# Moving the e operand and the SwiGLU hidden layer by 64 bytes in on-chip memory

## The reference, cut to what matters

```
h = rmsnorm(x, g_ffn1);  x = x + 0.5 * ((silu(h @ w1_a) * (h @ w3_a)) @ w2_a)
h = rmsnorm(x, g_mix);   p = h @ w_in            # 8 blocks for the branches, 3 x 1024 gate columns
merged = gate0 * fourier + gate1 * conv + gate2 * pool
x = x + merged @ w_o
h = rmsnorm(x, g_ffn2);  x = x + 0.5 * ((silu(h @ w1_b) * (h @ w3_b)) @ w2_b)
```

## The kernel before

| tensor | role | bytes past a multiple of 512 |
|---|---|---|
| w_hi, w_lo | stationary (ring) | 128 |
| xf_hi, xf_lo | moving, 256 columns | 192 |
| e_hi, e_lo | stationary | 192 |
| g_hi, g_lo | moving, 512 columns; stationary in time_spectra | 192 |
| xg_hi, xg_lo | moving, 512 columns | 128 |
| pf_hi, pf_lo | stationary, or moving in 512 columns | 128 |

## Time and profile before

### The profile page before, as it was taken

The page is one execution under the profiler, slowest core; times in us unless marked ns, Lnnn a source line. Parts: engine busy times, 40 slices in busy tenths (PEclk is TensorE's granted clock), DMA queues, the critical chain, the costliest instruction groups (busy, mean ns, idle before and its releaser), DMA issues.

```text
span 2904.9 us, 42557 instructions
## 1 busy us (share of the span) xinstructions
PE 2835.7 (98%) x16336; PEld 2473.3 (85%) x16336; DVE 2164.7 (75%) x2935; ACT 1504.2 (52%) x2001; POOL 512.7 (18%) x501
## 2 busy tenths in 40 slices
PE   9997999999969999999999999999999999999998
PEld 6686888888859999888889999899998888899997
DVE  6637999999978777666568776887776665687776
ACT  6834788888855444333235444454444332354443
POOL 3212111211111111111113111121111111131111
PEclk9998999999989999999999999999999999999999
DMA  5153999999946554332325656365543323266561
GB/s 221 44 181 131 354 387 385 382 383 388 390 129 174 159 169 134 104 101 94 104 94 148 180 146 180 96 167 161 166 137 102 100 96 102 96 154 172 151 177 58
DMA packets 171601, 515.31 MB, mean 177 GB/s; under 512 B 23808, under 2 KB 24320, under 8 KB 171136
## 3 DMA queue, kind: packets, MB, share of 16 engines
q1 hardware_dynamic: 129600, 422.38, 40.1%
q0 software_dynamic: 39872, 79.74, 13.3%
q10 hardware_dynamic: 1920, 10.38, 0.9%
HBM read 506.10 MB, written 23.07 MB: 182 GB/s over the span
## 4 chain that ended last, share of the span: by engine, by line
PE 85%; DVE 5%; issue 4%; DMA 3%; ACT 2%; POOL 1%; SPq 0%; ACTq 0%; DVEq 0%; POOLq 0%
PE bank L619 28%; PE bank L617 28%; PE bank L618 28%; DVE w_lo L1781 1%; PE bank L623 1%; ACT w_hi L1149 1%; DMA r_rows<-ye,hidx 1%; DMA sums<-in_w_a 0%; DMA raw<-in_w_b 0%; DMA sums<-in_w_b 0%; DMA raw<-in_rec_in 0%; POOL mv L1599 0%; POOL w_lo L1564 0%; PE bank L680 0%; DVE ft L2186 0%
## 5 line engine op out<-in xcount | busy, mean ns | idle before, releaser
L1781 DVE TENSOR_TENSOR w_lo<-raw,w_hi 128x1024 fp32r<-128x1024 f32 (+3 forms) x481 | 592.4, 1251 | 276.0 <-ACT w_hi L1149 270.3
L1149 ACT ACTIVATE w_hi<-raw 128x1024 fp32r<-128x1024 f32 (+1 forms) x491 | 507.3, 1045 | 289.8 <-PE bank L619 272.2
L617 PE MATMUL bank<-xf_hi,w_lo 128*128 128x256 f32 x2112 | 589.0, 279 | 8.9 <-DVE w_lo L1781 6.5
L619 PE MATMUL bank<-xf_hi,w_hi 128*128 128x256 f32 x2112 | 585.2, 277 | 0.0
L618 PE MATMUL bank<-xf_lo,w_hi 128*128 128x256 f32 x2112 | 585.1, 277 | 0.0
L617 PEld LDWEIGHTS bank<-xf_hi,w_lo 128*128 128x128 f32 x2112 | 397.2, 188 | 14.5 <-issue 10.4
L618 PEld LDWEIGHTS bank<-xf_lo,w_hi 128*128 128x128 f32 x2112 | 397.3, 188 | 2.4 <-issue 1.0
L619 PEld LDWEIGHTS bank<-xf_hi,w_hi 128*128 128x128 f32 x2112 | 397.1, 188 | 0.0
L619 PE MATMUL bank<-g_hi,w_hi 128*128 128x512 f32 x832 | 327.5, 394 | 0.0
L618 PE MATMUL bank<-g_lo,w_hi 128*128 128x512 f32 x832 | 325.6, 391 | 0.0
L617 PE MATMUL bank<-g_hi,w_lo 128*128 128x512 f32 x832 | 324.0, 389 | 0.3 <-DVE g_lo L2228 0.3
(11 more groups left out here) (366 smaller groups left out, 5278.2 us busy)
## 6 DMA issues: line engine op xcount, KB each, us to landing
raw_more<-in_moe SPq DMA_DIRECT2D x249, 512.0 KB, 7.2
raw<-in_moe SPq DMA_DIRECT2D x135, 512.0 KB, 7.1
raw<-in_w_a SPq DMA_DIRECT2D x77, 512.0 KB, 6.3
raw<-in_w_b SPq DMA_DIRECT2D x76, 512.0 KB, 6.4
raw<-in_w_in SPq DMA_DIRECT2D x73, 512.0 KB, 3.7
sums<-in_w_a POOLq DMA_DIRECT2D x88, 256.0 KB, 4.8
sums<-in_w_b POOLq DMA_DIRECT2D x88, 256.0 KB, 4.7
raw<-in_w_a SPq DMA_DIRECT2D x68, 256.0 KB, 5.5
```

The costliest lines, as they stand in the source:

```text
L617: e.matmul(out, a_lo, b_hi, start=start, stop=False, skip_group_check=partial)
L619: return e.matmul(out, a_hi, b_hi, start=False, stop=stop, skip_group_check=partial)
L1149: e.activation(split_of(k)[0], source_of(k), ACT.Copy).then_inc(s["hi"], 1)
L1781: e.tensor_tensor(lo, source_of(k), hi.bitcast(F32), ALU.subtract).then_inc(s["lo"], 1)
```

## The change

g_hi and g_lo start 64 bytes earlier, since the pad of 16 floats ahead of them is gone and the pad behind them has 16 floats more. e_hi and e_lo start 64 bytes earlier, since their pad now stands behind them. Both lie 128 bytes past a multiple of 512 after it. All other tensors stay where they are. No instruction is added, removed or moved.

```
-        sb("pad_g", [P, 16])
         g_hi = sb("g_hi", [P, 8, T], F32R)
         g_lo = sb("g_lo", [P, 8, T], F32R)
-        sb("pad_late", [P, 112])
+        sb("pad_late", [P, 128])
         raw_late = sb("raw_late", [P, NLATE, W])
...
             sums = sb("sums", [P, 2, W], into=ffn)
-            sb("pad_e", [P, 16], into=ffn)
             e_hi = sb("e_hi", [P, 2, T], F32R, ffn)
             e_lo = sb("e_lo", [P, 2, T], F32R, ffn)
+            sb("pad_e", [P, 16], into=ffn)
             with ExitStack() as up_only:
                 uu = sb("uu", [P, 2, 2, T], into=up_only)
```

## The result

The changed kernel takes 2924.53 us (median of 5 runs, 2919.03 to 2927.57) against 2909.04 us (5 runs, 2907.07 to 2912.03). The ratio is 1.0049, with an interval of 1.0037 to 1.0062, so the change makes the kernel slower by 0.37 to 0.62%. The forecast was 2924.

What follows compares the result with a forecast made beforehand. PE, busy 98% of the span, bounds the kernel by matmul count times pace. Ring +21.1 + 1.3, e -2.1, g -5.7 + 1.0 make +15.6 us on 2909, so 2924 us; range 2907 to 2929.

Steps and rivals of the forecast that it cites:

- Equal and 64 apart as what sets the pace: PE's two operands at the same remainder or 64 bytes apart: 256 columns 119.6 against 113.3 or 117.8 ns, 512 226.7 against 229.0.
- The ring stays slow behind an equal g block: SwiGLU matmuls with the ring stationary, xf moving: behind g at 128, 117.8 instead of 113.3 ns, +21.1 us; chance 0.70.
- the fast pace: SwiGLU matmuls of 256 columns, ring stationary: 113.3 ns start to start, against 117.8 slow; 4680 ring matmuls have it before.
- one narrow alignment of the weight load with the stream: PE's ring matmuls: what 113.3 ns looks like, with 117.8 ns as what all other entries end in.
- A changed e does not mend: In the SwiGLUs, e at 128 is just another ring block and no longer returns a slow stream to 113.3 ns.
- The sum: Whole kernel: ring +21.1 + 1.3, e -2.1, g -5.7 + 1.0, together +15.6 us.
- The 300 of the first stretches: Some 300 fast ring matmuls in the SwiGLUs' broken first stretches, all taken as lost: some 1.3 us.
- the entry of a block: At the start of each of 36 g blocks in the SwiGLUs, 0.03 us lost, 1 us in all.
- The writes of DVE and ACT: ACT's and DVE's writes of g and e, moved by 64 bytes, cost nothing; 75 us or more of room in 335.
- The time spectra at 0: 120 time-spectra matmuls with g stationary, equal instead of 64 apart: taken as nothing, -0.4 to +0.8 us kept.
- What the prediction said of now: In the SwiGLUs before the change, a g block mostly hands on the pace it gets, fast or slow.
- The rival of survival: In the SwiGLUs, equal g blocks leave the ring at 113.3 ns, as an equal e block does: 2898 us; chance 0.16.

Runs made afterwards that it cites:

- experiment 4: Against the kernel before, only g moved to 128, with e left at 192: 2922.3 us, ratio 1.0043.
- experiments 1 to 3: Against the kernel before, only e moved to 128, with g left at 192: 2917.37 us, ratio 1.0014; profiled three times at 2913.36, 2914.58 and 2912.66 us.
- experiment 7: Against the kernel before, e at 192 in steps 0 to 4 of each SwiGLU and at 128 from step 5, g at 192: 2905.82 us, ratio 0.9986.
- experiment 8: Against the changed kernel, g at 64, so 64 bytes below the ring's stationary tensor: 2937.74 us in one run.

## Why the prediction was right

*Equal and 64 apart as what sets the pace.* Right for this change. e's records fell from 283 to 279 and g's from 394 to 390 when their places alone moved. The Trainium skill ("SBUF — State Buffer", Who interferes with whom) gives PE two read ports and calls them independent. By that, as the prediction has it, neither term would exist and the time would stay at 2909 us. The runs do not agree: with the same instructions, nine placements took from 2909 to 2940 us. As a rule for other distances, though, "equal or not" is too coarse: 512 columns have 226.7 ns at 0, 229.0 at +64 and 232.5 to 233.3 at -64, +128 and +192.

*The ring stays slow behind an equal g block.* Right, and it was the step with the weakest support. It was argued from a difference of 0.02 us between five starts, and from the picture of the fast pace as "one narrow alignment of the weight load with the stream". No run shows such an alignment. g alone (experiment 4) shows it: a fast stream goes into 30 of 32 g blocks, and a slow one comes out of all. In the changed kernel itself only one of the 32 was entered fast. No run gives a reason, though, why an equal block of 256 columns mends and one of 512 breaks.

*A changed e does not mend.* Right (experiments 1 to 3: no e block changes the pace except where a wait stands at its end). In the changed kernel both moves act, but the second adds little once the first has broken the pace in every step. By the medians g alone costs 12.1 us and both together 15.5. The 3.4 us more are worked out as 3.1: g alone has 1410 fast ring matmuls in its profiled run, 768 of them (24 a step) behind the mending e block, against 233, which is 1177 x 4.5 = 5.3 us, less the 2.2 us that e gains.

*The sum.* Forecast +15.6, measured +15.5 by the medians. By its terms: 4987 ring matmuls outside waits had the fast pace before and 233 have it now, which makes 4754 x 4.44 = +21.1 where I had +21.1 + 1.3. The 300 of the first stretches were counted as all lost, and some of those steps are still fast. e: 1056 x 2.1 = -2.2, where I had -2.1. g: the pace is 226.7 and the entry of a block costs 0.03 to 0.04 us (10.91 or 10.92 against 48 x 0.22667 = 10.88; five starts take 1.16 us from 995.81 to 996.97), so -5.7 + 1.3 where I had + 1.0. This makes +14.5. That the median came within 1 us of the forecast is luck in part, since single executions of the changed kernel differ by more than that. The busy time of PE in the two profiled runs differs by 17.1 us, and their spans by 20.5: that pair has 2.8 us more idle time ahead of the ring's first line. It was 8.9 us in the kernel before:

```profile
L617 PE MATMUL bank<-xf_hi,w_lo 128*128 128x256 f32 x2112 | 589.0, 279 | 8.9 <-DVE w_lo L1781 6.5 <-issue 1.9 <-DVE uu L2273 0.2
```

It is 11.7 now, half of the difference from waits for DVE's xT at a pass's start. Five runs of the changed kernel differ by 8.5 us, so I take this for the spread between executions; it was not tested.

*The writes of DVE and ACT.* That they cost nothing was right: their busy times moved by 1.1 and 0.1 us. The limit given for it was too strict, though, as the room of 75 us in 335 is 29% of DVE's 259.5 us and not a tenth.

*The time spectra at 0.* Right, though by less of a rule than I had. With g as the stationary side a form of them has 283 ns after:

```profile
L618 PE MATMUL bank<-w_hi,g_hi 128*128 128x256 f32 x16 | 4.5, 283 | 0.0
```

The same form (line 619) had 283 before as well, at 64 apart:

```profile
L619 PE MATMUL bank<-w_hi,g_hi 128*128 128x256 f32 x16 | 4.5, 283 | 0.0
```

The distance there was -64, and these short series gave no 276 or 279. So pf's 283, which I read as a sign of "equal", was weaker evidence than the prediction made of it; what carries the reading is that e's own records moved with its place.

*What the prediction said of now.* "A block of g, as it is now, mostly hands on what it gets" was right for the fast stream and wrong in part for the slow one: six of twelve slow streams came out of the first g block fast (experiments 1 to 3), and so did one of three in the profiled run of the kernel before. This is why e alone took 2917 us and not the 2929 that I expected. It also corrects the reading of the earlier trace rows: the e block often mends, but the first g block at 192 may as well.

*The rival of survival.* Its price stands: with the pace kept, each SwiGLU is worth 6.0 us, and e alone reaches 2901.3 us in its best run, which was not profiled. It fell because its one condition, that the g block leave the stream fast, was met in none of 32 blocks.

## What to carry over

Where one engine's stream sets the time and its records of one shape have two values, compare paces from start to start in stretches. Ask of each block in the stream both what its own pace is and what pace it leaves behind, since here a block that was 0.7% faster by itself cost the next 120 ring matmuls 4% each (144 where e no longer mends). Move one operand at a time: the move of g was the loss, and the move of e was a gain once it was confined to the steps in which the stream was fast. And profile several executions of a kernel whose times spread more than its neighbours' (24 us against 5 to 15), because the mean over its executions may be a mixture of distinct cases.

## What the runs showed of the hardware

Paces by the distance of the moving operand's start from the stationary one's, modulo 512 bytes, as these kernels had it:

| distance, bytes | 256 columns, ns | 512 columns, ns |
|---|---|---|
| 0 | 119.6 to 120.0 | 226.7 |
| +64 | 113.3 or 117.8 | 229.0 |
| -64 | 113.3, 114.0 or 117.8 | 233.3 |
| +128 | 118.6 or 120.0 | 232.5 |
| +192 | not tried | 233.1 |

The short series of the time spectra are not in it: with the ring moving and g stationary at -64, the 256-column ones had some 120.8 ns. So the distance alone does not fix a pace. The ring never moved, either, so for 512 columns the distance can't be told from the moving operand's own place.

The pace is a property of the stream and not of the instruction alone. It lasts over more than a thousand ring matmuls, across blocks of g and e (944.4 to 1173.6 us at 276 ns in experiment 7, 945.4 to 1179.8 at 279 in the changed kernel). Where it changed, it did so at a block with another distance or column count, or at or just behind a wait, with one exception: in experiment 8, at 1592.7 us, the ring went from 117.8 to 113.3 ns some 50 matmuls behind the last wait. The window from 940 to 1185 us (its length, busy us of PE, PEld, DVE, ACT, POOL, then PEclk) in the kernel after:

```profile
940.00:1185.00 245.00, 245.00 (x1727) 229.85 (x1726) 178.25 (x274) 109.29 (x161) 32.53 (x42) 1.00 0.54 152
```

and before:

```profile
940.00:1185.00 245.00, 245.00 (x1739) 228.79 (x1739) 180.15 (x275) 111.67 (x164) 32.52 (x42) 1.00 0.53 153
```

The granted clock is full (1.00) in both, and PE does 12 matmuls fewer in the same time, so the clock is not the cause. What in PE's reads makes the two paces was not found.
